# Inverting the RWKV chunks in 32x32 diagonal blocks, with one joining step

## The reference, cut to what matters

```python
def _rwkv7_step(state, inp):
    r_t, w_t, k_t, v_t, kk_t, kka_t = inp
    sa = jnp.einsum('bhvk,bhk->bhv', state, -kk_t)
    state = state * w_t[:, :, None, :] + sa[..., None] * kka_t[:, :, None, :] + v_t[..., None] * k_t[:, :, None, :]
    return state, jnp.einsum('bhvk,bhk->bhv', state, r_t)
```

## Time and profile before

| | us |
|---|---|
| median of 3 runs | 1837.48 |
| lowest, highest | 1836.63, 1839.95 |
| the profiled execution, its own time | 1840.72 |
| its span, first to last instruction | 1838.9 |
| layer 0, level 1 of the inversion to the scan | 201.16 to 252.27 |
| layer 1, level 1 of the inversion to the scan | 805.01 to 853.40 |
| the expert stage | from about 985 to the end |

### The profile page before, as it was taken

The page is one execution under the profiler, slowest core; times in us unless marked ns, Lnnn a source line. Parts: engine busy times, 40 slices in busy tenths (PEclk is TensorE's granted clock), DMA queues, the critical chain, the costliest instruction groups (busy, mean ns, idle before and its releaser), DMA issues.

```text
span 1838.9 us, 64800 instructions
## 1 busy us (share of the span) xinstructions
PE 1746.3 (95%) x29342; PEld 1537.1 (84%) x29342; DVE 729.6 (40%) x1818; ACT 367.4 (20%) x858; POOL 2.9 (0%) x12
## 2 busy tenths in 40 slices
PE   7999988999999999998899999999999999989997
PEld 6887876577777788797758999999999998989986
DVE  6976736211020397674525222222222221222224
ACT  5443412011000554331302000000000000000001
POOL 0000000000000000000000000000000000000000
PEclk9999999999999999999998999999999999999999
DMA  8323211624434333322174999999999999999994
GB/s 311 119 96 115 93 48 60 234 107 147 161 140 156 138 115 106 112 81 71 47 309 186 393 425 426 427 426 426 426 425 427 425 425 414 407 384 425 426 425 208
DMA packets 55111, 473.28 MB, mean 257 GB/s; under 512 B 5280, under 2 KB 5568, under 8 KB 20960
## 3 DMA queue, kind: packets, MB, share of 16 engines
q1 hardware_dynamic: 53456, 463.49, 62.9%
q10 hardware_dynamic: 1184, 5.75, 0.8%
q0 software_dynamic: 368, 2.64, 0.4%
HBM read 470.80 MB, written 1.06 MB: 257 GB/s over the span
## 4 chain that ended last, share of the span: by engine, by line
PE 77%; DMA 15%; issue 3%; DVE 3%; ACT 2%; SPq 0%; DVEq 0%; ACTq 0%
PE bank L1094 17%; DMA ring<-in_moe 15%; PE bank L866 11%; PE bank L1014 9%; PE bank L539 9%; PE bank L916 8%; PE bank L936 4%; PE bank L898 3%; PE bank L880 3%; PE bank L700 2%; PE bank L1041 2%; PE bank L1084 1%; PE bank L689 1%; PE bank L679 1%; PE bank L518 1%
## 5 line engine op out<-in xcount | busy, mean ns | idle before, releaser
L1094 PE MATMUL bank<-arena,ring 128*64 128x80 f32 (+2 forms) x8192 | 305.8, 232 | 21.1 <-DMA ring<-in_moe 12.4
L1094 PEld LDWEIGHTS bank<-arena,ring 128*64 128x64 f32 x8192 | 290.3, 137 | 28.2 <-issue 14.7
L2069 DVE TENSOR_TENSOR arena<-arena,bank 128x80 f32<-128x80 f32 (+2 forms) x224 | 52.9, 236 | 515.8 <-ACT arena L1384 515.8
L1384 ACT ACTIVATE arena<-bank 128x80 f32<-128x80 f32 (+3 forms) x246 | 61.2, 249 | 894.7 <-PE bank L1094 706.3
L866 PE MATMUL bank<-xT,ring 128*128 128x256 f32 x1024 | 227.8, 381 | 0.0
L1094 PE MATMUL bank<-arena 128*64 128x80 f32 (+2 forms) x6144 | 223.2, 232 | 0.5
L866 PEld LDWEIGHTS bank<-xT,ring 128*128 128x128 f32 x1024 | 193.0, 190 | 30.3 <-issue 4.7
L1094 PEld LDWEIGHTS bank<-arena 128*64 128x64 f32 x6144 | 214.8, 137 | 3.1 <-DMA arena<-in_moe 1.0
L1014 PE MATMUL bank<-arena,ring 128*64 128x80 f32 (+2 forms) x4096 | 163.4, 232 | 4.0 <-issue 4.0
L539 PE MATMUL bank<-xT,ring 128*128 128x256 f32 x704 | 157.5, 385 | 8.0 <-DMA ring<-in_w_in 8.0
L1014 PEld LDWEIGHTS bank<-arena,ring 128*64 128x64 f32 x4096 | 153.6, 137 | 8.6 <-issue 4.4
(11 more groups left out here) (414 smaller groups left out, 1547.7 us busy)
## 6 DMA issues: line engine op xcount, KB each, us to landing
ring<-in_moe SPq DMA_DIRECT2D x128, 1536.0 KB, 16.0
arena<-in_moe SPq DMA_DIRECT2D x96, 1536.0 KB, 15.2
ring<-in_ffn SPq DMA_DIRECT2D x22, 1536.0 KB, 6.4
ring<-in_w_gate SPq DMA_DIRECT2D x32, 1024.0 KB, 4.9
ring<-in_w_in SPq DMA_DIRECT2D x14, 1536.0 KB, 6.7
ring<-in_w_branch SPq DMA_DIRECT2D x8, 1024.0 KB, 4.9
ring<-in_w_out SPq DMA_DIRECT2D x8, 1024.0 KB, 6.6
arena<-ml_rows ACTq DMA_DIRECT2D x4, 512.0 KB, 4.3
```

Source lines behind the costliest of these rows:

```text
L1094: last = mm(bank[c:c + STRIP, g * CAP:g * CAP + n], w[:, at:at + STRIP], rhs[:, kt, 0:n], start=(kt == 0), stop=(kt == KT - 1), skip_group ...
L1384: f(ff_sl[:, i % 2, 0:n], bank[:, 0:n], ACT.Silu).then_inc(S["h_silu"], 1)
L2069: tt_(ACTIVE_H[:, i, 0:PLACES[e]], ff_sl[:, s % 2, 0:PLACES[e]], bank[:, CAP:CAP + PLACES[e]], ALU.mult)\
```

## The change

The inverse is kept as its 32x32 diagonal blocks alone up to level 4. `rw_X`, `rw_CT` and `rw_P` become 128 partitions x 16 x 32 (the partition tells which of the two blocks of a matrix a row belongs to), with `rw_XB` for the transposed side and `rw_CB` for the compact triangular blocks, built once at level 0 by two new VectorE instructions a direction (L1711, L1712, with a constant `half` that is 1 on one half of each matrix's rows). The masks become 32 columns wide, five levels instead of six. A level's product is made of 32x32 matmuls on four array tiles in turn, twice as many of them; what ScalarE copies and VectorE masks, adds and transposes is 256 elements a partition instead of 512. At level 5 the new function `join_halves` makes the one off-diagonal 32x32 block of each matrix: both directions in one bank, 32 matmuls, one copy, 32 matmuls. It takes the off-diagonal block of `rw_MM` straight as an operand, with no mask. VectorE spreads `rw_XB` into the 64-wide `rw_XT` (two instructions of 512 elements) and adds the joining block to its corner (two of 256).

```diff
@@ masks and constants @@
-                  ("lmask", 12 * CH), ("reset", T), ("win", 2 * 3 * P), ("before", P),
+                  ("lmask", 10 * HB), ("reset", T), ("win", 2 * 3 * P), ("before", P),
...
+    put("half", np.stack([p % CH < HB, p % CH >= HB], 1))
@@ TensorE, rwkv @@
+                    if lev == 5:
+                        join_halves(L)
+                        continue
                     for d in range(2):
...
                         for m in range(8):
-                            for h in (0, 64):
-                                last = mm(b[h:h + 64, m * 64:(m + 1) * 64], rw_CT[h:h + 64, 8 * d + m, :],
-                                          rw_X[h:h + 64, 8 * d + m, :], start=True, stop=True)
+                            for r in range(0, P, HB):
+                                last = mm(b[r:r + HB, m * HB:(m + 1) * HB], rw_CT[r:r + HB, 8 * d + m, :],
+                                          rw_X[r:r + HB, 8 * d + m, :], start=True, stop=True)
                         fill(last)
...
+            def join_halves(L):
+
+                lanes = [(m, d, h + HB * d, h + HB * (1 - d)) for m in range(8) for h in (0, 64) for d in range(2)]
+                pe.wait_ge(S["rw_X"], 10 * (L + 1))
+                b = open_bank(("rwP", L, 5), "rw_P")
+                for m, d, at, to in lanes:
+                    last = mm(b[to:to + HB, m * HB:(m + 1) * HB],
+                              rw_MM[at:at + HB, 2 * d + m // 4, m % 4, 0, to % CH:to % CH + HB],
+                              rw_X[at:at + HB, 8 * d + m, :], start=True, stop=True)
+                fill(last)
+                pe.wait_ge(S["rw_P"], 9 * (L + 1))
+                b = open_bank(("rwQT", L, 5), "rw_XT", 12 * (L + 1))
+                for m, d, at, to in lanes:
+                    last = mm(b[at:at + HB, m * HB:(m + 1) * HB], rw_P[to:to + HB, m, :], rw_XB[to:to + HB, 8 * d + m, :],
+                              start=True, stop=True)
+                fill(last)
@@ ScalarE, rwkv @@
-                        step(nc.scalar.copy(flat(rw_P[:, 8 * d:8 * d + 8, :]), b[:, :]), "rw_P")
+                        step(nc.scalar.copy(flat(rw_P[:, 8 * d:8 * d + 8, :]), b[:, 0:8 * HB]), "rw_P")
+                    if lev == 5:
+                        b = bank_of(act, ("rwP", L, 5))
+                        step(nc.scalar.copy(flat(rw_P[:, 0:8, :]), b[:, 0:8 * HB]), "rw_P")
@@ VectorE, rwkv @@
+                        if lev == 0:
+                            src = rw_MM[:, 2 * d:2 * d + 2, :, 0, :].rearrange("p q c t -> p (q c) t")
+                            step(ts(rw_CB[:, own, :], src[:, :, 0:HB], C("half", 0, 1), None, ALU.mult))
+                            step(stt(rw_CB[:, own, :], src[:, :, HB:CH], C("half", 1, 1), rw_CB[:, own, :], ALU.mult,
+                                     ALU.add))
+                        step(tt_(rw_CT[:, own, :], rw_CB[:, own, :], bc(C("lmask", (5 * d + lev) * HB, HB), 1, 8),
+                                 ALU.mult), "rw_CT")
...
+                for k in range(2):
+                    ins = ts(rw_XT[:, :, k * HB:(k + 1) * HB], rw_XB[:, :, :], C("half", k, 1), None, ALU.mult)
+                step(ins)
+                beside(L, 5)
+                b = bank_of(dve, ("rwQT", L, 5))[:, 0:8 * HB].rearrange("p (m c) -> p m c", m=8)
+                for d in range(2):
+                    corner = rw_XT[:, 8 * d:8 * d + 8, (1 - d) * HB:(2 - d) * HB]
+                    step(stt(corner, b, C("half", d, 1), corner, ALU.mult, ALU.add), "rw_XT", hold=d == 1)
```

More of the change, by code:

```diff
@@ L31 @@
 CH = 64
+HB = CH // 2
 NCH = T // CH
@@ L116, in constants @@
     lm = []
+    j, i = (p % HB)[:, None], np.arange(HB)[None, :]
     for d in range(2):
-        for lev in range(6):
+        for lev in range(5):
             s = 1 << lev
@@ L123, in constants @@
     put("lmask", np.concatenate(lm, 1))
+    put("eye32", j == i)
+    put("half", np.stack([p % CH < HB, p % CH >= HB], 1))
     put("reset", np.broadcast_to((t % CH != 0), (P, T)))
@@ L307, in encoder @@
         rw_MM = area(13088, 4, NCH, 4, CH)
-        rw_X, rw_XT = area(17184, 16, CH), area(18208, 16, CH)
-        rw_P = rw_cin.rearrange("p a b -> p (a b)").rearrange("p (m c) -> p m c", m=16)
-        rw_CT = rw_cex.rearrange("p a b -> p (a b)").rearrange("p (m c) -> p m c", m=16)
+        rw_X, rw_XB, rw_XT = area(17184, 16, HB), area(17696, 16, HB), area(18208, 16, CH)
+        rw_P, rw_CB, rw_CT = area(4352, 16, HB), area(4864, 16, HB), area(5376, 16, HB)
         rw_S2 = area(4352, 2, 4, HD)
@@ L1684, in level_blocks @@
                             bank_of(dve, ("rwP", L, lev - 1, d))
-                        dst = rw_CT[:, 8 * d:8 * d + 8, :]
-                        src = rw_MM[:, 2 * d:2 * d + 2, :, 0, :].rearrange("p q c t -> p (q c) t")
-                        step(tt_(dst, src, bc(C("lmask", (6 * d + lev) * CH, CH), 1, 8), ALU.mult), "rw_CT")
+                        own = slice(8 * d, 8 * d + 8)
+                        if lev == 0:
[3 more added lines that the diff above has]
+                                     ALU.add))
@@ L1689, in rwkv @@
+                        step(tt_(rw_CT[:, own, :], rw_CB[:, own, :], bc(C("lmask", (5 * d + lev) * HB, HB), 1, 8),
+                                 ALU.mult), "rw_CT")
                 level_blocks(0)
-                for lev in range(6):
+                for lev in range(5):
                     for d in range(2):
-                        x, xt = (flat(a[:, 8 * d:8 * d + 8, :]) for a in (rw_X, rw_XT))
+                        x, xt = (flat(a[:, 8 * d:8 * d + 8, :]) for a in (rw_X, rw_XB))
                         if lev:
@@ L1694, in rwkv @@
                             b = bank_of(dve, ("rwQT", L, lev, d))
-                            step(tt_(xt, b[:, :], xt, ALU.add), "rw_XT")
+                            step(tt_(xt, b[:, 0:8 * HB], xt, ALU.add), "rw_XT")
                         else:
-                            step(tt_(rw_XT[:, 8 * d:8 * d + 8, :], rw_CT[:, 8 * d:8 * d + 8, :], bc(C("eye64"), 1, 8),
+                            step(tt_(rw_XB[:, 8 * d:8 * d + 8, :], rw_CT[:, 8 * d:8 * d + 8, :], bc(C("eye32"), 1, 8),
                                      ALU.add), "rw_XT")
-                        if lev < 5:
-                            step(nc.vector.transpose(x, xt), "rw_X")
@@ L1701, in rwkv @@
-                    if lev < 5:
-                        if lev == 0:
-                            level_blocks(1)
-                            beside(L, 0)
-                            beside(L, 1)
-                        else:
-                            beside(L, lev + 1)
-                            level_blocks(lev + 1)
+                        step(nc.vector.transpose(x, xt), "rw_X")
+                    if lev == 0:
+                        level_blocks(1)
+                        beside(L, 0)
+                        beside(L, 1)
+                    elif lev < 4:
+                        beside(L, lev + 1)
+                        level_blocks(lev + 1)
```

21 lines of the change are left out of this document (9 added, 12 removed).

## The result

The changed kernel takes 1853.83 us (median of 4 runs, 1850.49 to 1856.17) against 1837.06 us before in the same job (1834.11 to 1839.95): ratio 1.0093, 95% interval 1.0077 to 1.011. It is slower by 17 us where 15 us less was forecast, and the time lies outside the range of 1815 to 1846. The profiled execution took 1850.49 us, its span 1848.7 us.

The account below looks back on a forecast made before the run. TensorE, busy 95% of the span, was taken as the bound. Terms of -2.2, -0.8, -0.3 and -4.4 us made -7.7 a layer, -15.4 in all: 1825.3 from the profiled 1840.7, 1822 as median; range 1815 to 1846.

Parts of the forecast that it names:

- TensorE's own time: Levels' products: 128 pairs on four tiles take 1.28 us instead of 1.87, bounds 0.94 and 3.7 us.
- Rival 2: Levels 1 to 4 and join: instructions can't be fed fast enough; +19 us, 1856; chance 0.22 for 1834 to 1860.
- sign to look for: Instruction feeding too slow: about 3.9 us a product, with ScalarE and VectorE idle more than before.
- break-even of 9 ns an instruction: Feeding pace where gain turns to loss; above 7.3 each ns costs some 2 us a layer, against 3.5 gained.
- The argument against it: Against slow feeding: the longest fast stretches (15.4 and 14.6 ns) follow the columns, so look bound by the array.
- Level 0: Two more VectorE instructions a direction, at most 1.2 us later, hidden before level 1's products: cost 0.
- Level 3's second product: Bound by table load, tanh and copy: starts 0.2 us earlier, is 0.6 shorter, -0.8 us a layer.
- Level 4's mask: VectorE's mask ahead of level 4's first product: 0.42 instead of 0.69 us, -0.27 us a layer.
- The tail: From level 4's first product to the scan: 7.3 us instead of 11.71, -4.4 us a layer.
- The clock: Layer 0's low clock in levels 4 and 5 (2.7 us) left as is; 3 us either way in the range.
- Rival 1: Levels' products: a round costs 59 ns whatever its size; only -7 us, 1830.5; chance 0.25 for 1826 to 1833.
- Rival 3: Experts: the weights' stream is paced from elsewhere and absorbs the gain as longer DMA waits; 1837, chance 0.08.

Follow-up runs that it names:

- e6: The changed kernel with all four gates' large matmuls split around the products and the mLSTM rows' transposes ahead of level 4's gate: 1821.33 us, ratio 0.9911.
- e1: The changed kernel with its 32x32 matmuls reordered so that two array tiles take turns instead of four: 1852.72 us, ratio 1.009.
- e7: e6 with the weight transfers of the gates of levels 1 to 4 also held until the level is through: 1816.31 us, ratio 0.9880.
- e5: e4 with the gates of levels 3 and 4 cut in pieces between products, mLSTM rows' transposes ahead of level 4's gate: 1829.84 us, ratio 0.9955.
- e4: The kernel before with only the change's joining step at level 5, levels 1 to 4 staying 64 wide: 1832.03 us, ratio 0.9977.
- e9: The probe: the kernel before with 1024 extra, unused 32x32 matmuls on four tiles behind layer 0's level 5: 1898.63 us in one run.

## Why the prediction was wrong, step by step

**The step that failed** is the one on TensorE's own time, where it treats feeding as a uniform rate and sets that rate aside. It asked only how many nanoseconds a pair takes, between 0.94 and 3.7 us a product, and took 1.28. The product did take 1.35 us, within the forecast's own test ("about 1.3 us plus 0.2"), and 1.26 us from start to start. The pace was right to 2%, and it is not what a level costs. Two products issued in 2.6 us empty what is at hand, and a level then waits 3.51 to 4.76 us for the next block. From the first product's start to the end of the second, level 1 takes 208.51 - 201.40 = 7.1 us, levels 2 and 3 take 7.65 and 7.94; forecast were 2 x 1.28.

**Rival 2** had the right place and, nearly, the right size (1856), through the wrong mechanism. It priced 256 instructions at 14.6 ns each, 7.5 us for two products; the probe's mean of 14.1 ns says that this was near for a long burst, though by luck, since the 14.6 came from matmuls that the array paced. But its sign to look for, 3.9 us a product, is not in the trace, and its break-even of 9 ns an instruction doesn't exist: at 4.5 ns the kernel loses, and with the products apart (e6) it gains at the same 4.5 ns. What decides is the number of instructions in the time that a block takes to come, not the pace. The argument against it, that the 15.4 ns of the earlier trace rows follow the columns, was the weak link. It was right about the rows and wrong about what they allow: a stretch that the array paces says nothing of how instructions would come if the array were faster. That 15.4 ns lies a tenth above the probe's 14.1 is chance. The experts run in a loop (`pe.Fori`), and the trace of before shows that their instructions don't come in again: from 1050 to 1510 us queue 8 moves no packet, while TensorE runs 25,119 instructions:

```profile
1050.00:1510.00 460.00, 455.25 (x12561) 444.79 (x12558) 126.46 (x457) 40.99 (x144) 0.00 (x0) 1.00 1.01 426
```

That is some 1400 for each pass of the loop (25,119 in 18 passes, an estimate from the 126 expert weight loads of that stretch, seven a pass). So TensorE can keep more than two blocks. "Two at hand" says how far ahead of it they come in straight code.

The Trainium skill bears on this in two places. The page Runtime: NRT & Kernel Launch, section Instruction fetch mechanics, says that instructions are refilled in blocks of 16 KiB, 256 instructions, by the sequencer's own queue: the runs agree, 16 KB and 128 pairs a block. It also calls the cost mostly hidden, because a floor of about 20 cycles an instruction makes issue slower than the refill; the runs disagree, at 4.5 ns an instruction and stalls of 3.5 to 4.8 us. The prediction used that page only for the floor and passed over its blocks. By the Trainium skill's page TensorEngine Tiling (section Instruction Overhead), as the prediction read it, a product would have stayed at 1.87 us. The trace disagrees: it took 1.26 us from start to start on four tiles, and on two tiles a 32x32 pair starts every 14 ns (e1) where a 64x64 pair takes 30. That page of the Trainium skill speaks of columns only; here the weight load was halved as well.

**Part by part.** Level 0 cost nothing, as taken: level 1's first product comes straight behind the gate (201.40). Level 3's second product waits 1.24 us for ScalarE where 0.54 stood, since the first is shorter: as the working says, its copy is bound by the tanh. Level 4's mask is 0.88 us for both directions (forecast 2 x 0.42); the wait on it went from 1.28 to 1.01, by the 0.27 forecast. The tail was sized 7.3 and measured 8.19 and 8.49. Of the 0.9 and 1.2 us missed, 0.88 and 0.82 are stalls in the join's first product, the same failed step; the transposes (0.45 for 0.44), corners (2 x 0.44 for 2 x 0.42) and copies (0.37) came as worked out, and the spreading (0.88 for two) lay under the join. So outside the stalls the forecast of 15 us of gain had its mechanisms right; with the stalls mostly removed (e7) the gain is 1.2%, though e7 also profits from the gates that cover old waits, some 0.2% by e5 against e4 (0.9955 and 0.9977, barely clear of the noise).

**The clock.** 3 us either way were allowed. It fell to 0.82 and 0.84 over the whole stretch. The three gates of levels 2 to 4 alone lost (8.24 + 8.94 + 9.07) - (7.07 + 2 x 7.17) = 4.8 us in layer 0, and the first chunk of the scan took 7.0 us (261.76 to 268.75), where the same took 5.3 before (252.27 to 257.56).

**Rival 1** (59 ns a round) is refuted by the 1.35 us. **Rival 3** (the weights' stream absorbs it) is refuted too: over eleven versions (all but e9) layer 1's scan start went from 832.26 to 888.99, and the median followed, 1809.85 to 1869.87. Microseconds were passed through, as the prediction took it.

**The ways the step could have been caught.** The trace of before counts the instruction queue's packets on its page, and a level's two products are 512 instructions in 2.6 us by the forecast's own pace: two packets' worth, with weight transfers released right ahead. It also has the sign itself, small: in layer 1's scan TensorE stops for 1.00 us in the middle of identical matmuls, with nothing that releases it.

```profile
853.40 4.21 PE L700 MATMUL bank<-arena 64*64 64x64 f32 x126 [0.91 <-issue]
858.61 0.79 PE L700 MATMUL bank<-arena 64*64 64x64 f32 x18 [1.00 <-issue]
```

## What to carry to other kernels

Count TensorE's instructions in every few microseconds, not only their pace: weight load and matmul records both count, and float32 doubles them. Between 262 (e9) and 508 instructions (level 1) of a burst went at the array's speed, by where in a block it began; behind that, plan with 3 to 4 us for each 256 in straight code, and with 5.5 to 6.3 us when a transfer of a megabyte is under way (an estimate: the changed kernel's stalls plus the 1.26 us in which the block ahead is used, and in level 3 the wait of 1.24). If a change makes matmuls smaller and more, put the bursts between large matmuls, and start transfers outside them; here the same matmuls went from +0.9% to -1.4% by that, some 0.2% of it from old waits that the gates now cover. The experts' loop, which brings in nothing again, suggests another way; no run here tried it.

## What the runs showed of the hardware that was not expected

- 32x32 float32 matmuls on four tiles in turn start every 9 ns with their weight loads (128 in 1.35 us); on two tiles every 14 ns (1.90 us); 64x64 on two tiles every 30 ns (128 in 3.95 us).
- A long burst gets 256 instructions each 3.5 to 4.0 us, though a block's packet takes only 0.9 to 1.4 us on its queue and TensorE uses it in 1.9 us (e9). Each packet starts only 1.05 to 1.55 us after TensorE has begun the piece ahead. Why it does not start sooner is open.
- A loop of some 1400 instructions runs for 460 us without an instruction packet (the kernel before, experts).
- A block that comes while 1 MB of weights lands is about 2.5 us later (layer 0: stalls of 4.26, 4.63, 3.51 us against 1.89, 2.06, 0.98 with the loads held).
- TensorE's granted clock stays at 0.50 through the 46 us of e9's burst from 260 us on, and is 1.00 through the same kind of matmuls between gates (e6).
